# Where the matmul's moving tiles start in on-chip memory: 64 bytes past the weights by a period of 512, not 192

## The reference, cut to what matters

```
def swiglu(x, w_gu, w_down):
    gate, up = jnp.split(x @ w_gu, 2, axis=-1)
    return (jax.nn.silu(gate) * up) @ w_down

x = x + 0.5 * swiglu(rms_norm(x, ffn1_norm[l]), ffn1_w_gu[l], ffn1_w_down[l])
h = rms_norm(x, mix_norm[l]) @ a_w_in[i]          # the mixer of the layer
...
x = x + jnp.concatenate([o_a, o_m], axis=-1) @ w_out[l]
x = x + 0.5 * swiglu(rms_norm(x, ffn2_norm[l]), ffn2_w_gu[l], ffn2_w_down[l])
```

## Time and profile before

| | |
|---|---|
| time, median of 3 | 2906.02 us (2902.66 to 2908.01) |
| the profiled execution's own time | 2903.93 us |
| its span, first to last instruction | 2902.1 us |
| granted TensorE clock, mean | 0.994 |
| PE busy | 2815.7 us, 97% |
| DVE busy | 1796.4 us, 62% |
| ACT busy | 1491.8 us, 51% |
| DMA engines busy, mean | about 52%, 169 GB/s |

### The profile page before, as it was taken

The page is one execution under the profiler, slowest core; times in us unless marked ns, Lnnn a source line. Parts: engine busy times, 40 slices in busy tenths (PEclk is TensorE's granted clock), DMA queues, the critical chain, the costliest instruction groups (busy, mean ns, idle before and its releaser), DMA issues. The chain is left out here.

```text
span 2902.1 us, 47309 instructions
## 1 busy us (share of the span) xinstructions
PE 2815.7 (97%) x20443; PEld 2626.7 (91%) x20443; DVE 1796.4 (62%) x2467; ACT 1491.8 (51%) x2011; POOL 26.5 (1%) x41
## 2 busy tenths in 40 slices
PE   8999999999999999999999999999999999999999
PEld 7998878999986999999998998989999899998898
DVE  5558756556666656555578665466556655656655
ACT  6447445455454545443675634355454544544643
POOL 1000000000000000000001000000000000000000
PEclk9999999999998999999999999999999999999999
DMA  7555115555542555555453446555555555554653
GB/s 238 186 176 162 44 44 185 188 169 182 189 162 72 190 189 196 189 188 174 145 177 103 142 168 200 189 174 186 189 182 179 168 188 187 184 190 149 196 189 130
DMA packets 370110, 489.12 MB, mean 169 GB/s; under 512 B 15424, under 2 KB 329186, under 8 KB 369776
## 3 DMA queue, kind: packets, MB, share of 16 engines
q1 hardware_dynamic: 368944, 485.90, 51.6%
q0 software_dynamic: 640, 0.20, 0.0%
q10 hardware_dynamic: 320, 0.01, 0.0%
HBM read 485.02 MB, written 1.05 MB: 167 GB/s over the span
## 5 line engine op out<-in xcount | busy, mean ns | idle before, releaser
L884 PE MATMUL work<-input_hi,weights_hi 128*128 128x256 f32 x3424 | 964.4, 282 | 1.9 <-DVE weights_lo L251 1.8
L886 PE MATMUL work<-input_lo,weights_hi 128*128 128x256 f32 x3424 | 961.2, 281 | 0.0
L887 PE MATMUL work<-input_hi,weights_lo 128*128 128x256 f32 x3424 | 961.0, 281 | 0.0
L241 DVE TENSOR_TENSOR weights_lo<-weights_raw,weights_hi 128x2048 fp32r<-128x2048 f32 (+2 forms) x282 | 629.4, 2235 | 309.9 <-ACT weights_hi L221 309.3
L887 PEld LDWEIGHTS work<-input_hi,weights_lo 128*128 128x128 f32 x3424 | 655.7, 192 | 0.0
L884 PEld LDWEIGHTS work<-input_hi,weights_hi 128*128 128x128 f32 x3424 | 644.1, 188 | 6.5 <-DVE weights_lo L251 2.2
L886 PEld LDWEIGHTS work<-input_lo,weights_hi 128*128 128x128 f32 x3424 | 643.3, 188 | 3.8
L225 ACT ACTIVATE weights_hi<-weights_raw,params 128x512 fp32r<-128x512 f32 (+2 forms) x736 | 462.0, 701 | 324.3 <-DMA weights_raw<-in_ffn_w_gu 160.3
L221 ACT ACTIVATE weights_hi<-weights_raw 128x2048 fp32r<-128x2048 f32 (+2 forms) x282 | 524.1, 1865 | 158.6 <-DMA weights_raw<-in_ffn_w_up 94.6
L251 DVE SCALAR_TENSOR_TENSOR weights_lo<-weights_raw,params,weights_hi 128x512 fp32r<-128x512 f32 (+2 forms) x736 | 492.6, 732 | 169.6 <-ACT weights_hi L225 169.5
L344 PE MATMUL acc<-weights_hi,hidden_hi 128*128 128x512 f32 x880 | 344.7, 392 | 8.3 <-DVE hidden_lo L1060 6.3
(11 more groups left out here) (565 smaller groups left out, 3461.9 us busy)
## 6 DMA issues: line engine op xcount, KB each, us to landing
weights_raw<-in_ffn_w_gu SPq DMA_DIRECT2D x176, 512.0 KB, 4.7
weights_raw<-in_ffn_w_in SPq DMA_DIRECT2D x176, 512.0 KB, 4.8
weights_raw<-in_ffn_w_down SPq DMA_DIRECT2D x66, 1024.0 KB, 4.9
weights_raw<-in_w_in SPq DMA_DIRECT2D x44, 1024.0 KB, 5.1
weights_raw<-in_ffn_w_out SPq DMA_DIRECT2D x44, 1024.0 KB, 4.9
weights_raw<-in_a_w_in SPq DMA_DIRECT2D x29, 1024.0 KB, 5.5
weights_raw<-in_ffn_w_gate SPq DMA_DIRECT2D x44, 512.0 KB, 3.7
weights_raw<-in_ffn_w_up SPq DMA_DIRECT2D x44, 512.0 KB, 4.7
```

Source lines behind the costliest of these rows:

```text
L241: last = self.nc.vector.tensor_tensor(self.wl[:, n % SLOTS, 0:kc * cols], raw, self.wh[:, n % SLOTS, 0:kc * cols].bitcast(F32), ALU.subtract)
L884: nc.tensor.matmul(o, wh[:, k, ms], K.hi[:, c, :], start=(c == 0 and m == 0), stop=False, skip_group_check=True)
L886: nc.tensor.matmul(o, wh[:, k, ms], K.lo[:, c, :], start=False, stop=False, skip_group_check=True)
L887: last = nc.tensor.matmul(o, wl[:, k, ms], K.hi[:, c, :], start=False, stop=(c == DC - 1), skip_group_check=True)
```

## The change

One constant: the remainder of the tiles that `home(MOVING)` places falls from 320 to 192.

```
-MOVING, STATIONARY = 320, 128
+MOVING, STATIONARY = 192, 128
```

## The result

The changed kernel takes 2909.78 us (median of 12 runs, 2905.39 to 2914.87) against 2903.70 us for the kernel before (12 runs, 2898.59 to 2908.01): a ratio of 1.0018, 95% interval 1.0010 to 1.0027. It is slower, by about 5 us (3 to 8), where 2924 us was predicted, 18 us more than the 2906.02 us that were known of before. The sign was right, the size was not.

The account below looks back on a forecast made before the run. PE was taken as the bound: number of matmuls by the pace at which they start. The profiled 2903.9 us + 18 + 0 + 0 gave 2922 us, 2924 us as the median of runs; 8-in-10 range 2868 to 2948 us.

Parts of the forecast that it names:

- The paces before: Column matmuls on PE: 117.8 or 113.4 ns at difference 192, 120.0 at 0; 12,000 at the long pace, 2,000 short.
- the third rival: Column matmuls: difference 64 costs like 0, 120.0 ns throughout and no short pace; +39 us, 2945 us, chance 0.14.
- Step 1: The 12,000 long-pace column matmuls go to 119.3 ns at difference 64, 1.5 ns more each: +18 us.
- Both signs of being wrong: Column matmuls at or below 117.8 ns, or the kernel's time moving while their pace doesn't.
- Step 2: The 2,000 column matmuls at the short pace stay at 113.4 ns: 0 us; +13 us if they go to 120.0.
- Step 3: Matmuls with weights moving and input stationary, difference 320 to 448: taken as 0, bounds -4 and +3 us.
- Step 4: The ffn's 3 x 880 row matmuls keep both addresses and stay at 226.7 ns: 0 us.
- Step 5: DVE and ACT: their tiles shift by 128 bytes too, but their work is hidden behind PE: 0 us.
- The rule weighed: PE's separate read ports for moving operand and weight loads: the address could not matter, sum 0, 2906 us.
- Flat: Column matmuls: only a coinciding start costs more, 64 bytes away is clear; no change, 2906 us, chance 0.22.
- All at the short pace: Column matmuls fall into 113.4 ns, -4.4 ns x 12,000 = -53 us: 2853 us, 2880 with half; chance 0.30 for part or all.
- Like the difference 0: Column matmuls: 64 is inside the bad place, 120.0 ns and the short pace gone; +39 us, 2945 us, chance 0.14.

Follow-up runs that it names:

- e2: Changed kernel with input_hi and input_lo put back at remainder 320, the other moving tiles at 192; 2904.3 us, ratio 1.0000 to the kernel before.
- e3: Kernel before with MOVING = 128, so difference 0 between moving and stationary start for all column matmuls; 2940.8 us, ratio 1.0131.
- e11: Kernel before with the first column matmul behind the 512-wide rows of an ffn step issued as two of 128 columns; 2881.6 us, ratio 0.9922.
- e9: Kernel before with MOVING = 352, difference 224 for the column matmuls; 2927.3 us, ratio 1.0079.
- e13: Changed kernel (MOVING = 192, difference 64) with the first column matmul behind the rows issued as two of 128 columns; 2921.4 us, ratio 1.0059 to the kernel before.
- e8: Kernel before with weights, moving and stationary tiles all 64 bytes higher, every difference as before; 2906.3 us, ratio 1.0005.

## Why the prediction was right or wrong

**What bounds the kernel.** Right, as far as it was tried: the losses and gains above are found in PE's starts, and moving the tiles of DVE and ACT alone (e2) cost nothing.

**The paces before.** Right: 113.4, 117.8 and 120.0 ns are real levels, and e3 put the whole kernel at the last of them, 2940.8 us against the 2945 that the third rival worked out for it. The 2,000 matmuls at the short pace, taken from mean records, were 2,582 by their starts.

**Step 1, the price at 64.** This is the step that failed: "Straight between them 64 gives 120.0 - 2.2 x 64 / 192 = 119.3 ns, 1.5 ns more". Measured 117.8 ns in all 90 steps, no more at all; the term of +18 us is 0. A straight line was laid between two points of a quantity that repeats: in their mean pace the differences 0 and 128 are one, and so are 64 and 192. What makes it repeat stays open. Both signs of being wrong that the prediction named came: the pace not above 117.8, and a time that moved without it. The rows at 192 and 320 with one pace were in hand, 128 apart, and were given to a rival with 0.22. That the kernel did get slower, as forecast, is luck: the term that was to make it slower is 0, and the 5 us come from steps 2 and 4, which were taken as 0.

**Step 2, the matmuls at the short pace.** "They stay at 113.4 in my forecast, 0 us." Half of them did not: +5.9 us between the two traces, which is most of the loss, though how many are short varies at one difference too. They went to 117.8 and not to 120.0 ns, so the measured cost lies between the two bounds (0 and +13 us), of which one was taken.

**Step 3, weights moving.** Taken as 0, within -4 to +3; measured -2.1 and +1.3. Right in the sum. In its parts the 512-wide ones missed their bound: 3.5 ns more, to 233.2, where 2.3 was the bound and within 3 ns of 229.0 was foreseen.

**Step 4, the ffn rows.** "keep both addresses: 0". They cost +3.2 us. The sum priced each matmul by its own two addresses and had no term for the seam, where the first seven rows now start up to 240 ns apart.

**Step 5.** Right, e2.

**The rule weighed.** The rule of the Trainium skill ("TensorE: Matmul & The Clock Gate", section "Step-by-step: what each phase is for"), that loading weights takes nothing from a running matmul's reads, would have given 2906 us, 4 us from the measured time and nearer than the forecast. It can't be why: taken as the prediction took it, that the address could not matter, it leaves no room for e3, which is 38 us slower than before.

**The rivals.** *Flat* had the pace of the ffn right, its time within 4 us and inside its own range (2901 to 2911). Its reason, that only a start that coincides costs more, is wrong: 128 and 256 are as dear as 0. It also had no loss, where the runs show one of 3 to 8 us. *All at the short pace* was wrong for this change and right as a mechanism: another entry, not another distance, gives it (e11), at 192 and 448 and not at 64. *Like the difference 0* was wrong at 64 and describes 0 and 256, and in the mean 128.

## What to carry to other kernels

Read a matmul's pace from its starts, and look for stretches of the same line at two paces: where they exist at the same addresses, part of the gap between them may be had by the way PE enters a stretch. Here one matmul in two halves gave 23 us at the differences 192 and 448, more than moving a tile between two good addresses is worth (5 us), but the same edit cost 12 us at 64 (2921.4 against 2909.8), so it has to be tried at the address that is used. If addresses are to be set, sweep one full period in steps of half of what is suspected and never interpolate, and price the seams between shapes as well as the shapes.

## What was not expected of the hardware

- With 128 columns of 4 bytes as the stationary block and 256 as the moving one, the mean pace behind the rows goes by the difference of their starts by 128 bytes: 117.8 ns at 64, 118.3 at 96 (e9), 119.9 to 120.0 at 0, the same in all 90 steps of a trace. Below the mean, differences 256 apart are alike and those 128 apart are not: 120 ns each at 0 and 256, but 118, 120 and 122 in turn at 128.
- Behind the same entry (two halves) PE falls into 113.4 ns at 192 and 448 and into 117.8 at 64. Behind a wait it can be either at one difference and one place: at 64 it is 117.8 ns in the changed kernel and 113.4 in e13, and at 192 it is 117.8 before and 113.4 in e8, for 407 matmuls in a row from 1344 and 1345 us.
- A rhythm lasts. It holds for 96 matmuls and more (137 in the earlier trace rows, 407 in e8) and changes at a wait, at another shape, at another tile, or at one matmul in halves.
- The 24 rows behind long-pace columns take 5.44 us (192, 448) or 5.48 us (64, 320) by a tile address that none of them uses.
